# One core, two fused model blocks: how the tokens' quarters are laid over the partitions for the expert dots

## The chip, the cores and the metric

One core of a Trainium2 chip runs the whole program. The time is device microseconds of one execution, and a kernel's time is the median of its runs. The core has a tensor engine (PE: matrix products and turns, results in eight PSUM banks of 128 x 512 f32), a vector engine (VectorE, DVE), a scalar engine (ScalarE, ACT), GpSimd (POOL) and SyncE (SP), which work side by side and wait for each other by semaphores, and 16 DMA engines that move data between memory (HBM) and the on-chip SBUF.

## The reference, cut to what matters

256 tokens of width 1024 go through a first block of two layers and then a second block (latent attention and an mLSTM side by side, then a layer of experts). The change is in the experts:

```python
def one(xb):                                              # 128 tokens of h2, (128, 1024)
    q = (xb @ w_pq).reshape(128, 8, 2, 128)               # 8 heads, 2 halves
    s = einsum('thpd,hpkd->thpk', q, sub_keys)            # 128 scores per half
    sv, si = top_k(s, 16)                                 # then the best 16 of the 256 sums:
    best, pos = top_k(cand, 16); eidx = take(cidx, pos)   # 16 experts of 16384 per head and token
    g = softmax(best)
    act = gelu(einsum('thkd,td->thk', expert_u[eidx], xb))
    return einsum('thk,thkd->td', g * act, expert_v[eidx])
```

So each token meets 128 experts, and every expert row (u and v, 2 x 1024 f32, 8 KB) is fetched for one token. For 256 tokens that is 268 MB.

## The kernel before, in words

The tokens are two tiles of 128 (tt = 0 and 1). `first_*` and `mix_*` are the blocks up to the experts; `peer_*` is the expert part, one function per engine. Tile 0 enters the expert part while tile 1 is still in the mixers of the second block: `second_tile_at(g)` hands out tile 1's remaining steps, one or two with each batch g.

A turn k is one head of one tile (`TURNS`, 16 turns: heads 0 to 4 of tile 0, head 4 of tile 1, then both tiles by turns, at the end heads 0 to 3 of tile 1). For a turn PE makes the queries (`queries`, 16 products against `w_pq`) and the scores (`scores`, 2 products), each copied out of PSUM by ScalarE (`queries(k)` and `scores(k)` of `peer_scalar`), VectorE picks the best 16 (`halves`, `candidates`, `places`), PE spreads the list (`list_spread`) and VectorE copies it out (`listed`). GpSimd then gathers the expert rows with indirect DMAs (L3095). A turn has four batches of four gathers. One gather brings 128 rows of 8 KB, 1 MB, for 32 tokens: partition p of a gather belongs to token p % 32 of a quarter and to slot p // 32. Sixteen buffers `e_uv` are used in four places of four; places 2 and 3 come into use at batches 8 and 17 (`ROOM_AT`).

Each gather n of a batch is for quarter n of the tile's tokens. VectorE multiplies its u rows with the tokens and sums (`dots`, L2890), which needs the 32 tokens of a quarter repeated over the four groups of 32 partitions: these are the four tensors `m["h2q"][tt][q]`, each 128 x 1024. ScalarE makes gelu and a diagonal (`gelu`, `folded`, from the constant block `K["fold"]`), and PE adds the weighted v rows (`add`, `e_diag`).

The quarters come from `hT`, the normed tokens with the features on the partitions. `quarter_turned(tt, q)` (L2653) does for each half of the features 16 products of 128 x 32 by the identity, four for each of four feature tiles: each writes the same 32 tokens, turned, to one group of 32 partitions of a PSUM bank. `quarter_set` (L3004) copies the bank with ScalarE. For tile 0 three quarters stand in PE's order between the scores of turn 0 and the queries of turn 1, and the last one behind these (L2738 to L2742). For tile 1 they are the steps ("quarter", 0..3) of batches 15 to 18 (L2580); in a batch PE does them behind the batch's first add and ahead of the routing products that follow (L2758 to L2760). Tile 1's first turn is turn 5 (batches 20 to 23); its queries are in batch 14, its scores in batch 15, its list in batch 17. Turn 6's queries are in batch 17 behind the quarter, its scores in batch 18 behind the quarter, its list in batch 21 (`ROUTING_AT`). `dots` waits for the last copy of its quarter only in a tile's first turn (L2888).

The order of every engine's work is written out by hand in this way. Banks are taken in turn from a rotation (`c.banks.take`); PE waits until ScalarE or VectorE has emptied a bank. At the entry of the expert part the rotation is banks 2 and 3 (L1832), later 2, 3 and 7, from tile 1's output on again 2 and 3.

Of the kernel before, what the change touches and what calls it, by code (L numbers as in the profile page):

```python
# [57 lines left out]
def constants():  # L58

    p, f = np.arange(P)[:, None], np.arange(P)[None, :]  # L60
    t = np.arange(T).reshape(NT, P)
    n = np.arange(CMP_PAD)
    parts = {}
    parts["ident"] = np.eye(P)
    parts["zeros"] = np.zeros((P, P))
    parts["lower"] = np.where(f <= p, 0.0, NEG)
    parts["upper"] = np.where(f >= p, 0.0, NEG)
    ok = (n[None, None] < NCMP) & (n[None, None] * S_CMP + L_CMP - 1 <= t.T[:, :, None])
    parts["cmp_neg"] = np.where(ok, 0.0, NEG).reshape(P, -1)
    parts["cmp_one"] = ok.astype(float).reshape(P, -1)  # L70
    parts["blocks"] = (np.arange(P)[:, None] // CMP_PAD == np.arange(HEADS)[None]).astype(float)
    inv = (np.float32(10000.0) ** (-np.arange(0, HD, 2, dtype=np.float32) / np.float32(HD)))
    parts["inv_freq"] = np.broadcast_to(inv, (P, HD // 2))
    half = ROPE2 // 4
    inv2 = np.float32(10000.0) ** (-np.arange(half, dtype=np.float32) * np.float32(2.0 / (2 * half)))
    ang = np.stack([(t // 64).T, (t % 64).T], -1).astype(np.float32)[..., None] * inv2
    parts["cos2"] = np.cos(ang).reshape(P, -1)
    parts["sin2"] = np.sin(ang).reshape(P, -1)
    parts["fold"] = (np.arange(P)[:, None] % SIDE == np.arange(SIDE)[None]).astype(float)
    parts["iota"] = np.broadcast_to(np.arange(TOPK), (P, TOPK))  # L80
    parts["ones"] = np.ones((P, P))
    at, where = 0, {}
    for name, a in parts.items():
        where[name] = (at, at + a.shape[1])
        at += a.shape[1]
    return np.concatenate(list(parts.values()), 1).astype(np.float32), where
# [2486 lines left out]
def second_tile_at(g):  # L2573
    work = [("values", g - 1)] if 1 <= g <= MLA_H else []
    work += [("attention", g)] if g < MLA_H else []
    work += [("outputs", g - 4)] if 4 <= g < 4 + ML_H else []
    work += [("levels", g - 3)] if 3 <= g < 3 + ML_H else []
    return work + {5: [("att_out",)], 6: [("att_turn",)], 7: [("out0", 0)], 8: [("out0", 1), ("summed", 0)],
                   9: [("gated", 0), ("summed", 1)], 10: [("turn", 0), ("gated", 1)], 11: [("turn", 1), ("out1", 0)],
                   12: [("out1", 1), ("mixed",)], 13: [("normed",)], 14: [("filled",)], 15: [("quarter", 0)],  # L2580
                   16: [("quarter", 1)], 17: [("quarter", 2)], 18: [("quarter", 3)]}.get(g, [])


def peer_memory(nc, stack, second, cond):
# [14 lines left out]
def peer_tensor(c, m, mix, K):  # L2599
# [1 line left out]
    bank_k, bank_q = c.banks.tiles[0:2]  # L2601
    acc = [c.banks.tiles[4:6], c.banks.tiles[6:8]]
    hT, ident = m["hT"], K["ident"]


    in_keys = []

# [42 lines left out]
        spread(bank_k[:, 2 * P:2 * P + BUFS], m["best"][:, k % 2], ("weight_spread", k))  # L2650
        in_keys[:] = [("weight_set", k)]

    def quarter_turned(tt, q):  # L2653

        tokens = slice(tt * P + q * SIDE, tt * P + q * SIDE + SIDE)
        for half in range(2):
            bank = take("h2q", tt, q, half)
            for k in range(4):
                for s in range(QUARTERS):
                    pe.mm(bank[s * SIDE:s * SIDE + SIDE, k * P:k * P + P], hT[:, 4 * half + k, tokens], ident,  # L2660
                          skip_group_check=True, tile_position=(0, s * SIDE),
                          tell=filled("h2q", tt, q, half) if (k, s) == (3, QUARTERS - 1) else None)

    def add(g, c0, c1):

# [48 lines left out]
    def mixers_after(step, *a):  # L2714
# [3 lines left out]
        elif step == "attention":  # L2718
            later.att_turned(*a)
            if a[0] + 1 < MLA_H:  # L2720
                later.att_scores(a[0] + 1)
        elif step == "out0":
            if a[0] == 0:
                c.banks.rotate(2, 3)
            later.mix_out(0, range(2 * a[0], 2 * a[0] + 2))
        elif step == "out1":
            later.mix_out(1, range(2 * a[0], 2 * a[0] + 2))
        elif step == "quarter":
            quarter_turned(1, *a)

    c.banks.leave(0)
    c.banks.leave(1)
# [2 lines left out]
    kept_busy(c, K, bank_q, 512, 256)  # L2735
    queries(0)
    scores(0)
    for q in range(QUARTERS - 1):  # L2738
        quarter_turned(0, q)
    queries(1)  # L2740
    quarter_turned(0, QUARTERS - 1)
    scores(1)  # L2742
    list_spread(0)
    weights_spread(0)
# [215 lines left out]
def peer_scalar(c, m, mix, K, x):  # L2960
# [36 lines left out]
    def folded(g):  # L2997

        k, batch = divmod(g, PER_TURN)
        for n in range(BATCH):  # L3000
            slot = batch * BATCH + n
            act.f(m["fold_w"][:, g % 2, n, :], K["fold"], ACT.Copy, scale=m["weight"][:, k % 2, slot:slot + 1], settled=n == 0)

    def quarter_set(tt, q):  # L3004
        for half in range(2):
            act.wait_ge(*c.full("h2q", tt, q, half))
# [37 lines left out]
    def mixers_late(step, *a):  # L3044
# [2 lines left out]
            later.att_turned(*a)  # L3047
        elif step == "mixed":
            later.squares()
        elif step == "quarter":  # L3050
            quarter_set(1, *a)

    first.filled(m["hT"], 0)
    queries(0)
    scores(0)
    for q in range(QUARTERS - 1):
        quarter_set(0, q)
    soft(0)
    queries(1)
    quarter_set(0, QUARTERS - 1)  # L3060
    scores(1)
    weighted(0)
    folded(0)
# [66 lines left out]
def parts_of(nc, keep, A, out, counted):  # L3130
# [3 lines left out]
    table = nc.alloc_sbuf_tensor("constants", [P, max(b for _, b in where.values())], F32)[:]  # L3134
    K = {name: table[:, a:b] for name, (a, b) in where.items()}
    zeros = where["zeros"][0]
    K["masks"] = table[:, zeros + P:zeros + 3 * P].rearrange("p (d t) -> p d t", d=2)
    K["wide"] = table[:, 0:4 * P]
    K["mask2"] = table[:, zeros:zeros + 2 * P]
# [106 lines left out]
```

## Time and profile before

| | us |
|---|---|
| median of 3 runs | 1372.97 (1371.43 to 1375.32) |
| profiled execution | 1378.54 |
| its span | 1377.1 |
| PE busy (share of the span) | 1031.6 (75%) |
| VectorE busy | 885.6 (64%) |
| ScalarE busy | 475.3 (35%) |
| GpSimd busy | 307.3 (22%) |
| gathers' queue, share of 16 DMA engines | 46.5%, 268.45 MB |

The profile is of one execution. Its times count from the span's start; the expert part begins at some 672 us. A busy share is an average over stages with different limits. In a row of a timeline the first number is the start, the second the time until the last of the merged instructions ended, then the engine, the line (often that of a helper, L169 for all products), the operation, what it writes and reads, the sizes, and in brackets how long the engine had been idle and what ended that. One f32 product leaves two MATMUL records, one turn leaves one. "issue" is idle time in which the engine waited for nothing that the profile shows; "remote" is a wait whose releaser the profile doesn't name.

### The profile page before, as it was taken

To read this page: it belongs to the slowest core of one execution; us is meant where nothing else is said; L and a number is where in the kernel's file an instruction comes from. 1 tells how busy PE (TensorE), PEld (TensorE's weight loads), DVE (VectorE), ACT (ScalarE), POOL (GpSimd) and SP (SyncE) were. 2 spreads that over 40 slices of the span, in tenths; PEclk is the share of its full clock that TensorE was granted. 3 is DMA by queue.
4 is the path that set the end of the run, shared out by engine and by line. 5 is a ranking of instruction groups with operands and counts; after the bars stand their busy time and mean duration, and the time that the engine had idled before them with its cause. 6 is when DMAs were issued, how large, how long until landed. Compare 5 with 4: busy or idle time off the path is not lost.

```text
span 1377.1 us, 17655 instructions
## 1 busy us (share of the span) xinstructions
PE 1031.6 (75%) x6291; PEld 590.1 (43%) x6291; DVE 885.6 (64%) x2281; ACT 475.3 (35%) x1312; POOL 307.3 (22%) x265
## 2 busy tenths in 40 slices
PE   7998999999899999999968787665434455443535
PEld 4776756577675647445534431332212222211201
DVE  5488643429864445845476798458866777777755
ACT  2013623101352521465347654333332233233321
POOL 0000000000000000000044444344435555443451
PEclk9999999999999999999989898876666666666667
DMA  8362453436237332145189999999999999999997
GB/s 305 132 223 92 160 214 130 183 105 249 93 131 281 117 104 93 62 183 203 55 358 426 409 426 427 425 412 368 426 426 426 426 426 426 427 426 426 427 426 306
DMA packets 56107, 391.14 MB, mean 284 GB/s; under 512 B 9931, under 2 KB 13055, under 8 KB 15955
## 3 DMA queue, kind: packets, MB, share of 16 engines
q0 software_dynamic: 37440, 268.45, 46.5%
q1 hardware_dynamic: 18578, 121.56, 23.9%
q8 instruction: 50, 0.82, 0.2%
q14 instruction: 39, 0.31, 0.1%
HBM read 387.89 MB, written 1.05 MB: 282 GB/s over the span
## 4 chain that ended last, share of the span: by engine, by line
DVE 21%; PE 16%; DMA 12%; ACT 5%; another core or an unknown queue 4%; issue 4%; POOL 1%; ACTq 0%; DVEq 0%
PE bank L169 16%; DMA e_uv<-in_experts_dram,e_listed 9%; DVE e_uv L2890 8%; DMA e_uv<-in_experts_dram,e_listed_uv 2%; DVE e_hot L185 1%; POOL e_uv L3095 1%; ACT e_diag L230 1%; DVE e_rest L2821 1%; ACT L230 1%; DVE e_e L210 1%; ACT m_W L230 1%; PE bank L174 1%; DMA m_w<-in_ada_dram 1%; DVE e_si L2825 1%
## 5 line engine op out<-in xcount | busy, mean ns | idle before, releaser
L3095 POOL DMA_INDIRECT e_uv<-in_experts_dram,e_listed x252 | 296.8, 1178 | 1035.3 <-DVE e_listed L202 806.9
L169 PE MATMUL bank<-e_uv,e_diag 128*32 128x512 f32 x1024 | 231.1, 879 | 285.0 <-ACT e_diag L230 254.5
L2890 DVE CUSTOM_DVE_ANT_0 e_uv<-e_uv,e_h2q 128x1024 f32<-128x1024 f32 x192 | 228.4, 1224 | 63.8 <-DMA e_uv<-in_experts_dram,e_listed 59.5
L169 PEld LDWEIGHTS bank<-e_uv,e_diag 128*32 128x32 f32 x1024 | 41.4, 140 | 409.7 <-ACT e_diag L230 283.5
L169 PE MATMUL bank<-hT,weights 128*128 128x256 f32 x640 | 141.0, 380 | 2.8 <-DVE hT L191 1.4
L169 PEld LDWEIGHTS bank<-hT,weights 128*128 128x128 f32 x640 | 120.8, 190 | 21.0 <-DVE hT L191 1.6
L230 ACT ACT_TABLE_LOAD x79 | 101.4, 1283 | 7.8 <-PE bank L169 1.7
L169 PE MATMUL bank<-weights,hT 128*128 128x512 f32 (+1 forms) x256 | 102.5, 557 | 1.7 <-DMA weights<-in_layer_q_dram 1.7
L197 DVE SCALAR_TENSOR_TENSOR conv<-ubuf,vec,conv 128x256 f32<-128x256 f32 x240 | 96.8, 480 | 0.6
L230 ACT ACTIVATE e_act<-e_dot 128x4 f32<-128x4 f32 (+1 forms) x81 | 16.6, 205 | 210.0 <-DVE e_dot L2890 200.7
L169 PE MATMUL bank<-weights,mixT 128*128 128x512 f32 x192 | 85.5, 598 | 2.4 <-DVE mixT L202 1.6
L2890 DVE CUSTOM_DVE_ANT_0 e_uv<-e_uv,e_hT 128x1024 f32<-128x1024 f32 x64 | 76.3, 1222 | 13.1 <-DMA e_uv<-in_experts_dram,e_listed 13.1
L169 PEld LDWEIGHTS bank<-e_hT,e_w_pq 128*128 128x128 f32 x512 | 62.0, 201 | 18.7 <-issue 18.2
L169 PEld LDWEIGHTS bank<-weights,hT 128*128 128x128 f32 x256 | 48.8, 194 | 49.4 <-issue 44.1
L230 ACT ACTIVATE e_diag<-cond_mod_rows,e_act 128x32 f32<-128x32 f32 x256 | 63.1, 311 | 8.1
L169 PE MATMUL bank<-e_hT,e_w_pq 128*128 128x128 f32 x512 | 65.2, 288 | 0.6 <-ACT e_hT L230 0.6
L2817 DVE MAX8 e_sv<-cond_mod_rows 128x8 f32<-128x128 f32 x32 | 9.4, 295 | 86.8 <-ACT cond_mod_rows L234 69.5
L230 ACT ACTIVATE cond_mod_rows<-constants,e_weight 128x32 f32<-128x32 f32 x256 | 61.3, 310 | 2.1
L169 PEld LDWEIGHTS bank<-weights,mixT 128*128 128x128 f32 x192 | 35.5, 190 | 45.4 <-issue 42.5
L185 DVE TENSOR_TENSOR x_sb<-bank,x_sb 128x512 f32<-128x512 f32 x16 | 11.1, 692 | 63.4 <-PE bank L169 63.4
L230 ACT ACTIVATE S<-S,mx 128x128 f32<-128x128 f32 (+1 forms) x64 | 29.1, 455 | 61.5 <-DVE mx L222 59.3
L169 PE MATMUL bank<-m_w,e_hT 128*128 128x464 f32 (+1 forms) x96 | 40.0, 569 | 1.2 <-PEq L3169 1.1
(385 smaller groups left out, 1429.5 us busy)
## 6 DMA issues: line engine op xcount, KB each, us to landing
weights<-in_ada_dram SPq DMA_DIRECT2D x8, 2048.0 KB, 8.7
weights<-in_layer_out_dram SPq DMA_DIRECT2D x6, 2048.0 KB, 8.1
e_w_pq<-in_w_pq_dram SPq DMA_DIRECT2D x12, 1024.0 KB
weights<-in_layer_cmp_dram SPq DMA_DIRECT2D x4, 2048.0 KB, 8.3
weights<-in_layer_q_dram SPq DMA_DIRECT2D x2, 2048.0 KB, 8.8
weights<-in_layer_kvc_dram SPq DMA_DIRECT2D x2, 2048.0 KB, 12.7
weights<-in_layer_gb_dram SPq DMA_DIRECT2D x2, 2048.0 KB, 15.1
weights<-in_layer_ga_dram SPq DMA_DIRECT2D x2, 2048.0 KB, 15.2
```

The source lines that it names most:

```text
L169: ins = self.engine.matmul(out, lhsT, rhs, start=start, stop=stop, **kw)
L174: ins = self.engine.transpose(out, a, ident)
L185: return self.mark(self.engine.tensor_tensor(out, a, b, op), tell)
L197: return self.mark(self.engine.scalar_tensor_tensor(out, a, s, b, op0, op1), tell)
L210: return self.mark(self.engine.tensor_reduce(out, a, AX.X, op), tell)
L230: return self.mark(self.engine.activation(out, a, func, **kw), tell)
L2817: dve.mark(c.nc.vector.max(out_v[:, 0:8], values))
L2821: dve.mark(c.nc.vector.match_replace(scratch, out_v[:, 0:8], values, -3e38))
L2825: return dve.mark(c.nc.vector.max_index(out_i[:, 8:16], out_v[:, 8:16], scratch))
L2890: dve.mark(c.nc.vector.tensor_tensor_reduce(u, u, h2q[tt][n], 1.0, 0.0, MUL, ADD, m["dot"][:, j:j + 1]), ("dots_set", g, c0) if n == c1 - ...
L3095: ins = c.nc.gpsimd.indirect_dma_start(out=to, out_offset=None, in_=rows, in_offset=bass.IndirectOffsetOnAxis(ap=of, axis=0))
```

## The change

The tile is turned back whole, once: `tokens_turned(tt)` makes eight 128 x 128 turns from `hT` into two banks, and ScalarE (`tokens_set`) copies them to `h2q[tt][3]`, the place of the last quarter. Then `quarter_spread(tt, q)` makes each half of each quarter with one product: the 32 token rows of the quarter (32 partitions, 512 columns) by 32 rows of a constant block that has a one wherever column and row agree modulo 32. The products of quarter 0 wait for ScalarE's copies. The constant block grows from 32 to 128 columns; `K["fold"]` is its first 32. In tile 1's steps batch 15 now has ("rows",) and the four quarters follow in batches 16 to 19. For tile 0 the rotation is set to banks 2, 3 and 7 ahead of the turns, two quarters stand ahead of the queries of turn 1 and two behind them, on PE and ScalarE alike.

```diff
--- before.py
+++ after.py
@@ -76,7 +76,7 @@
     ang = np.stack([(t // 64).T, (t % 64).T], -1).astype(np.float32)[..., None] * inv2
     parts["cos2"] = np.cos(ang).reshape(P, -1)
     parts["sin2"] = np.sin(ang).reshape(P, -1)
-    parts["fold"] = (np.arange(P)[:, None] % SIDE == np.arange(SIDE)[None]).astype(float)
+    parts["fold"] = (np.arange(P)[:, None] % SIDE == np.arange(P)[None] % SIDE).astype(float)
     parts["iota"] = np.broadcast_to(np.arange(TOPK), (P, TOPK))
     parts["ones"] = np.ones((P, P))
     at, where = 0, {}
@@ -2577,8 +2577,8 @@
     work += [("levels", g - 3)] if 3 <= g < 3 + ML_H else []
     return work + {5: [("att_out",)], 6: [("att_turn",)], 7: [("out0", 0)], 8: [("out0", 1), ("summed", 0)],
                    9: [("gated", 0), ("summed", 1)], 10: [("turn", 0), ("gated", 1)], 11: [("turn", 1), ("out1", 0)],
-                   12: [("out1", 1), ("mixed",)], 13: [("normed",)], 14: [("filled",)], 15: [("quarter", 0)],
-                   16: [("quarter", 1)], 17: [("quarter", 2)], 18: [("quarter", 3)]}.get(g, [])
+                   12: [("out1", 1), ("mixed",)], 13: [("normed",)], 14: [("filled",)], 15: [("rows",)],
+                   16: [("quarter", 0)], 17: [("quarter", 1)], 18: [("quarter", 2)], 19: [("quarter", 3)]}.get(g, [])
 
 
 def peer_memory(nc, stack, second, cond):
@@ -2601,7 +2601,7 @@
     bank_k, bank_q = c.banks.tiles[0:2]
     acc = [c.banks.tiles[4:6], c.banks.tiles[6:8]]
     hT, ident = m["hT"], K["ident"]
-
+    h2_rows = [m["h2q"][tt][QUARTERS - 1] for tt in range(NT)]
 
     in_keys = []
 
@@ -2650,16 +2650,23 @@
         spread(bank_k[:, 2 * P:2 * P + BUFS], m["best"][:, k % 2], ("weight_spread", k))
         in_keys[:] = [("weight_set", k)]
 
-    def quarter_turned(tt, q):
-
-        tokens = slice(tt * P + q * SIDE, tt * P + q * SIDE + SIDE)
+    def tokens_turned(tt):
+
+        for half in range(2):
+            bank = take("h2_rows", tt, half)
+            for k in range(4):
+                pe.turn(bank[:, k * P:k * P + P], hT[:, 4 * half + k, tt * P:tt * P + P], ident,
+                        tell=filled("h2_rows", tt, half) if k == 3 else None)
+
+    def quarter_spread(tt, q):
+
+        tokens = slice(q * SIDE, q * SIDE + SIDE)
         for half in range(2):
             bank = take("h2q", tt, q, half)
-            for k in range(4):
-                for s in range(QUARTERS):
-                    pe.mm(bank[s * SIDE:s * SIDE + SIDE, k * P:k * P + P], hT[:, 4 * half + k, tokens], ident,
-                          skip_group_check=True, tile_position=(0, s * SIDE),
-                          tell=filled("h2q", tt, q, half) if (k, s) == (3, QUARTERS - 1) else None)
+            if q == 0:
+                pe.wait_ge(*c.taken("h2_rows", tt, half))
+            pe.mm(bank[:, :], K["spread"][tokens, :], h2_rows[tt][tokens, half * 512:half * 512 + 512],
+                  tell=filled("h2q", tt, q, half))
 
     def add(g, c0, c1):
 
@@ -2725,8 +2732,10 @@
             later.mix_out(0, range(2 * a[0], 2 * a[0] + 2))
         elif step == "out1":
             later.mix_out(1, range(2 * a[0], 2 * a[0] + 2))
+        elif step == "rows":
+            tokens_turned(1)
         elif step == "quarter":
-            quarter_turned(1, *a)
+            quarter_spread(1, *a)
 
     c.banks.leave(0)
     c.banks.leave(1)
@@ -2735,10 +2744,13 @@
     kept_busy(c, K, bank_q, 512, 256)
     queries(0)
     scores(0)
-    for q in range(QUARTERS - 1):
-        quarter_turned(0, q)
+    c.banks.rotate(2, 3, 7)
+    tokens_turned(0)
+    quarter_spread(0, 0)
+    quarter_spread(0, 1)
     queries(1)
-    quarter_turned(0, QUARTERS - 1)
+    quarter_spread(0, 2)
+    quarter_spread(0, 3)
     scores(1)
     list_spread(0)
     weights_spread(0)
@@ -3001,6 +3013,12 @@
             slot = batch * BATCH + n
             act.f(m["fold_w"][:, g % 2, n, :], K["fold"], ACT.Copy, scale=m["weight"][:, k % 2, slot:slot + 1], settled=n == 0)
 
+    def tokens_set(tt):
+        for half in range(2):
+            act.wait_ge(*c.full("h2_rows", tt, half))
+            act.copy(m["h2q"][tt][QUARTERS - 1][:, half * 512:half * 512 + 512], c.banks.tile("h2_rows", tt, half),
+                     tell=c.banks.emptied("h2_rows", tt, half))
+
     def quarter_set(tt, q):
         for half in range(2):
             act.wait_ge(*c.full("h2q", tt, q, half))
@@ -3047,17 +3065,21 @@
             later.att_turned(*a)
         elif step == "mixed":
             later.squares()
+        elif step == "rows":
+            tokens_set(1)
         elif step == "quarter":
             quarter_set(1, *a)
 
     first.filled(m["hT"], 0)
     queries(0)
     scores(0)
-    for q in range(QUARTERS - 1):
-        quarter_set(0, q)
+    tokens_set(0)
+    quarter_set(0, 0)
+    quarter_set(0, 1)
     soft(0)
     queries(1)
-    quarter_set(0, QUARTERS - 1)
+    quarter_set(0, 2)
+    quarter_set(0, 3)
     scores(1)
     weighted(0)
     folded(0)
@@ -3134,6 +3156,7 @@
     table = nc.alloc_sbuf_tensor("constants", [P, max(b for _, b in where.values())], F32)[:]
     K = {name: table[:, a:b] for name, (a, b) in where.items()}
     zeros = where["zeros"][0]
+    K["spread"], K["fold"] = K["fold"], K["fold"][:, 0:SIDE]
     K["masks"] = table[:, zeros + P:zeros + 3 * P].rearrange("p (d t) -> p d t", d=2)
     K["wide"] = table[:, 0:4 * P]
     K["mask2"] = table[:, zeros:zeros + 2 * P]
```

## Rows read from the trace of the kernel before

**Rows 1.** the page: GB/s moved in each of 40 slices of 34.4 us
```profile
GB/s 305 132 223 92 160 214 130 183 105 249 93 131 281 117 104 93 62 183 203 55 358 426 409 426 427 425 412 368 426 426 426 426 426 426 427 426 426 427 426 306
```

**Rows 2.** busy time by window: engines (x instructions), PE clock, DMA share, GB/s
```profile
906.00:912.00 6.00, 4.89 (x62) 2.08 (x64) 6.00 (x12) 1.23 (x6) 4.71 (x4) 0.62 0.93 367
948.00:954.00 6.00, 2.85 (x16) 0.59 (x16) 5.90 (x12) 2.12 (x9) 3.37 (x2) 0.50 0.45 150
```

**Rows 3.** timeline of PE at the entry: start us, length us, instruction, [idle before]
```profile
671.47 1.09 PE L174 MATMUL bank<-constants,m_W 128*128 128x128 f32 x8 [0.23 <-DVE m_W L191]
679.22 4.21 PE L169 MATMUL bank<-constants,e_hT 128*32 128x128 f32 x143
684.76 1.58 PE L169 MATMUL bank<-constants,e_hT 128*32 128x128 f32 x49 [1.33 <-issue]
686.26 3.84 PE L169 MATMUL bank<-e_hT,e_w_pq 128*128 128x128 f32 x32
690.03 1.96 PE L169 MATMUL bank<-constants,e_hT 128*32 128x128 f32 x64
692.56 0.43 PE L169 MATMUL bank<-e_e,constants 128*32 128x4 f32 x32
694.81 1.12 PE L169 MATMUL bank<-m_krT,m_qrT 64*128 64x512 f32 x2
695.87 3.70 PE L169 MATMUL bank<-m_w,e_hT 128*128 128x512 f32 x8
```

**Rows 4.** timeline of ScalarE and VectorE in the same stretch
```profile
680.37 0.58 ACT L234 COPY e_hT<-bank 128x512 f32<-128x512 f32 x1 [0.67 <-PE bank L169]
688.33 0.21 ACT L230 ACTIVATE e_best<-e_gap 128x16 f32<-128x16 f32 x1
...
690.39 0.17 DVE L197 SCALAR_TENSOR_TENSOR e_e<-e_e 128x16 f32<-128x16 f32 x1
```

**Rows 5.** timeline of ScalarE and VectorE, batches 15 to 19
```profile
884.87 0.37 ACT L234 COPY cond_mod_rows<-bank 128x256 f32<-128x256 f32 x1
...
917.19 0.37 ACT L234 COPY e_qT<-bank 128x256 f32<-128x256 f32 x1 [0.73 <-PE bank L169]
928.72 0.37 ACT L234 COPY cond_mod_rows<-bank 128x256 f32<-128x256 f32 x1 [0.67 <-PE bank L169]
...
929.12 0.29 DVE L2817 MAX8 e_sv<-cond_mod_rows 128x8 f32<-128x128 f32 x1 [13.72 <-ACT cond_mod_rows L234]
```

**Rows 6.** timeline of PE, batches 14 to 19
```profile
860.95 1.97 PE L174 MATMUL bank<-constants,m_W 128*128 128x128 f32 x8
...
880.22 2.22 PE L169 MATMUL bank<-constants,e_hT 128*32 128x128 f32 x52
...
910.52 1.87 PE L169 MATMUL bank<-constants,e_hT 128*32 128x128 f32 x48
913.31 3.84 PE L169 MATMUL bank<-e_hT,e_w_pq 128*128 128x128 f32 x32
918.82 1.59 PE L169 MATMUL bank<-constants,e_hT 128*32 128x128 f32 x40
931.50 3.37 PE L169 MATMUL bank<-e_uv,e_diag 128*32 128x512 f32 x16 [2.82 <-ACT e_diag L230]
```

**Rows 7.** timeline of VectorE and GpSimd, batch 20 and turn 6's first gather
```profile
939.66 1.21 DVE L2890 CUSTOM_DVE_ANT_0 e_uv<-e_uv,e_h2q 128x1024 f32<-128x1024 f32 x1
...
950.33 1.74 POOL L3095 DMA_INDIRECT e_uv<-in_experts_dram,e_listed  x1 [8.64 <-DVE e_listed L202]
```

**Rows 8.** timeline of ScalarE in two later turns, query copy and score copy
```profile
1039.84 0.37 ACT L234 COPY e_qT<-bank 128x256 f32<-128x256 f32 x1 [3.38 <-PE bank L169]
...
1051.34 0.37 ACT L234 COPY cond_mod_rows<-bank 128x256 f32<-128x256 f32 x1
...
1157.94 0.37 ACT L234 COPY e_qT<-bank 128x256 f32<-128x256 f32 x1 [2.73 <-PE bank L169]
...
1164.99 0.37 ACT L234 COPY cond_mod_rows<-bank 128x256 f32<-128x256 f32 x1
```

## The prediction, made before the changed kernel was run

> **What bounds the kernel now.** I read the slices of the page first. From the 21st slice on (688 us) the DMA engines move 409 to 427 GB/s with one break, the 28th slice with 368 [rows 1]: the second half is the stream of expert rows that GpSimd gathers. It can end earlier in two ways only: it starts earlier, or it stands still for less time. So I asked windows where it stands still. There are two pockets: 906 to 912 at 367 GB/s and 948 to 954 at 150 GB/s [rows 2]. Against 426 they lose 6 x 59/426 = 0.8 us and 6 x 276/426 = 3.9 us, 4.7 us together. From the 29th slice to the 39th the rate is flat at 426 or 427.
>
> Then the timelines, to see what ends each wait of the gathers. The start: the first list of experts is spread by PE at 692.56 [rows 3], but VectorE had chosen the experts at 690.39 + 0.17 = 690.56 [rows 4]. PE was late by 2.0 us, since it ran tile 0's quarters, the queries and the scores of turn 1 first. The large pocket: GpSimd's first gather of turn 6 starts at 950.33 after 8.64 us of waiting for the list [rows 7]. Behind that list is one unbroken VectorE chain that began at 929.12 after 13.72 us of idling for the scores of turn 6 [rows 5], and those come from PE behind quarter 3. That quarter, 64 PE records, 1.96 us when undisturbed [rows 3], starts at 918.82 with 40 records [rows 6] and its scores are copied only at 928.72. The small pocket has the same form a turn earlier: quarter 0 starts at 880.22 in earnest [rows 6], the scores of turn 5 are copied at 884.87 [rows 5].
>
> **The entry, tile 0.** Before: 679.22 to 692.56 is 13.34 us [rows 3]. Quarters 0 to 2 with the gap of 1.33 us take 7.04, the queries 3.77 start to start, the last quarter and the scores 2.53. After: eight turns of 128x128 cost 1.09 us [rows 3]. The first spread waits for ScalarE to copy the first turned half, 0.58 us [rows 4]; half the turns are done after 0.55, so the copy ends 1.13 + about 0.25 of handing over after 679.22, some 0.3 us behind the turns. Then eight products, 32 rows deep, 128 columns out and 512 long. No row shows this shape. From below: four products of 512 columns in 3.70 us, less the tail of the last of some 0.26, is 0.86 each; from above: the product with 64 rows starts at 694.81 and the next one at 695.87, 1.06 each [rows 3]. A short depth earns nothing in these rows. I take 0.90, nearer to the run of like products, since both halves of a quarter are alike: 7.2 us. Note that this is about what a half cost before (1.96/2 = 0.98): the change removes PE records, 512 to 32 for the quarters of both tiles with 16 turns beside them, but hardly any PE time. Sum: 1.09 + 0.3 + 7.2 + 3.77 + 0.64 for the scores = 13.0, a gain of 0.3 us. At 0.86 it is a gain of 0.7, at 1.06 a loss of 0.9. The gap of 1.33 us, in which PE waited for nothing that the trace names, is left out of the new sum because the record-dense stretch in which it fell is gone; if it comes back, the entry loses 1.0 instead. The gain cannot pass 1.8 us, where VectorE's choice at 690.56 becomes the last one.
>
> ScalarE makes two more copies of 0.58 per tile. In the entry it idles before each copy [rows 4], so they are hidden, but its order now decides something: quarters 2 and 3 are copied behind the exponential of turn 0 (done at 688.6 [rows 4]) and behind the query copy. There are three banks for four spreads, so the fourth spread cannot start before about 689.8. By the sum PE reaches it at about 690.5: hidden, with 0.7 us of cover, and late next if PE got much faster.
>
> The Trainium skill, page "TensorE: Matmul & The Clock Gate", section "Part 3: Packing small matmuls — row/col tiling", says that products at different row groups run side by side in the array. Here the second half of a quarter and the first of the next would pair; no row of this trace has two neighbouring products at different row groups, so it neither agrees nor disagrees.
>
> **Tile 1, turn 5.** Batch 15 had quarter 0 in front of the scores: 880.22 to 883.83, 3.6 us [rows 6]. Now eight turns stand there, 1.09 us [rows 3] or 1.97 us when the granted clock is low [rows 6]; two ScalarE copies follow as before. That is 1.6 to 2.5 us on PE. ScalarE's two copies of the turned halves and the score copy follow within a microsecond of it. I take 1.5 us, since the few records after 882.4 came slowly for a reason that may stay (below: 0). From that copy on VectorE's chain to this list is unbroken, so list 5 moves by 1.5 and the small pocket of 0.8 us closes.
>
> **Tile 1, turn 6.** Three parts. First the 1.5 us are inherited, as the dots, the diagonals and the adds that precede the queries hang on the same chain. Second, batch 17 had quarter 2 in front of the queries, 910.52 to 913.31 or 2.8 us [rows 6]; quarter 1 now stands there as two spreads, 1.8 us at the high clock, twice that at half clock: a gain of 1.0 (bounds -0.8 and +1.1). Third, from the query copy to the score copy 917.19 to 928.72 is 11.5 us [rows 5]. The seven later turns to 1207 us have no quarter in this place, and still show 7.05 us in the shortest (1157.94 to 1164.99) and 11.50 in the longest (1039.84 to 1051.34) [rows 8]: the slow piece belongs mostly to the turn, not to the quarter. The middle of the two is 9.3; a quarter's two spreads remain in front of the scores, so I take 10.0, a gain of 1.5 (bounds: 0, and 4.5 at 7.05). Together the list of turn 6 comes 1.5 + 1.0 + 1.5 = 4.0 us earlier. The stream itself ran 0.8 us ahead, so 3.2 us of the second pocket's 3.9 close.
>
> **Moved and added.** Quarter 3 goes from batch 18 to 19 and the first dots of tile 1, in batch 20, need it. The fourth dot started at 939.66 [rows 7]. The new place is behind batch 19's add, 931.50 + 3.37 = 934.9 [rows 6]; two spreads at half clock, 1.8 each, end at 938.5 and ScalarE's last copy at 939.1. So it is just in time with nothing else moved; all of it moves together. Cover: 0.5 us. Queued behind on PE is only batch 20's add; on ScalarE it is the next exponential, which VectorE needs 4 us later. The wait of quarter 0 for the whole tile's copy is met a batch earlier, at nothing. The constants grow by 96 columns, 48 KB, 0.1 us at 426 GB/s at the kernel's start: counted as lost. ScalarE's weight fold reads the first 32 columns as before: nothing.
>
> **Sum.** 0.3 + 0.8 + 3.2 - 0.1 = 4.2 us. The profiled execution took 1378.54 us (span 1377.1), so it becomes 1374.3. It lies 5.6 us above the median of 1372.97; the pockets may be a little smaller in an execution without the profiler, but I have no row for that. Forecast: 1372.97 - 4.2 = 1368.8 us.
>
> **Rivals.**
> *Nothing is given back.* The slow piece is the turn's own and ScalarE and PE come out of it at the same instants. For it: 11.50 us in a turn without a quarter. Against it: the shortest of 7.05, and 3.6 us for quarter 0 where eight turns need 2. Only 0.3 at the entry and little elsewhere: 1372.4.
> *Everything is given back.* The spreads pair up in the array, which takes some 1.7 us (two of 0.86) off the eight and brings the entry to the bound of 1.8, and both pockets close: 1372.97 - 1.8 - 4.7 = 1366.5. That is what the page's rule of the row groups would make of the entry (by it the trace is silent).
> *Slower: the last quarter becomes the wait.* Spreads at 1.06 lose 0.9 at the entry, and the slow piece of a turn falls on batch 19's spreads, which have 0.5 us of cover. From there each microsecond holds the fourth dot of batch 20, list 6 behind it and the stream. Such a piece lasts up to 6 us; at 3 us the time is 1372.97 + 0.9 + 3 + 0.1 = 1377.0. It decides as soon as PE reaches quarter 3 later than about 935.5 on the old clock of events while the scores came no earlier.
>
> **Chances.** Forecast 0.45, nothing 0.25, everything 0.14, slower 0.16. About 0.3%, 4.1 us, is what a measurement of this kernel can tell from no change. Over half of the forecast's own spread (1366.5 to 1371.5) lies beyond it. Faster: 0.26 + 0.14 = 0.40; slower: 0.14 of the last case; the rest, 0.46, is the same within 0.3%. The range that leaves out 2 in 10 goes from 1365.0 to 1376.0.
>
> **What would show it.** Right: eight PE turns of some 1.1 us at 679 and no gap behind them; spreads 0.86 to 0.95 us apart; first list spread near 692.2; scores of turn 5 copied near 883.4 and of turn 6 near 924.5 on the same scale; 948 to 954 at over 400 GB/s. Wrong: spreads over 1.0 us apart; VectorE waiting for a copy of quarter 3 in batch 20; the score copy of turn 6 still 11 us behind its query copy; or the pocket closed and the end not earlier, which would say that the stream isn't what sets the end.

## The result: 1.006 times the time before, and the profile after

| | before | after |
|---|---|---|
| median, us | 1372.88 (1371.43 to 1375.32, 6 runs) | 1381.64 (1381.01 to 1382.56, 6 runs) |
| ratio after to before, 95% interval | | 1.006 (1.0049 to 1.007) |
| profiled execution, its span | 1378.54, 1377.1 | 1381.07, 1379.7 |
| mean granted clock of PE | 0.866 | 0.860 |

The forecast was 1368.8 us with a range of 1365 to 1376. The kernel is slower by 8.8 us, outside of the range and on the other side of no change.

From the page of the changed kernel: the GB/s in 40 slices, and the gathers' queue with its packets, MB and share of 16 DMA engines:

```profile
GB/s 306 138 216 92 167 211 126 183 114 240 93 142 270 116 122 75 62 183 220 58 376 420 405 421 422 420 421 420 421 421 421 421 420 420 421 419 422 421 421 275
...
q0 software_dynamic: 37440, 268.45, 47.0%
```

From the 24th slice to the 39th the rate is 419 to 422 GB/s, where [rows 1] had 425 to 427 outside of the pockets. The queue moves the same packets and bytes and holds the engines for 47.0% of a longer span (46.5% before). The 28th slice, with 368 in [rows 1] the visible pocket, now shows 420, like its neighbours. The windows of the changed kernel, with the columns of [rows 2]:

```profile
906.00:912.00 6.00, 3.54 (x48) 1.53 (x40) 3.39 (x5) 2.68 (x8) 4.06 (x4) 0.81 1.02 419
948.00:954.00 6.00, 0.00 (x0) 0.00 (x0) 1.31 (x4) 0.73 (x4) 2.76 (x3) 0.72 1.02 417
1000.00:1300.00 300.00, 133.31 (x1152) 57.67 (x1148) 211.35 (x521) 85.92 (x301) 123.43 (x113) 0.66 1.01 421
```

and of the kernel before, two windows that were not shown ahead of the prediction:

```profile
930.00:964.00 34.00, 17.69 (x164) 7.70 (x164) 28.15 (x69) 10.85 (x38) 17.06 (x12) 0.68 0.91 368
...
1000.00:1300.00 300.00, 133.82 (x1208) 58.45 (x1197) 214.31 (x543) 90.19 (x316) 140.32 (x120) 0.66 1.01 426
```

So both pockets of [rows 2] are closed (367 to 419 and 150 to 417 GB/s), as forecast, and the end is not earlier. (Whether it was the new order of work that closed them is a question of its own: see b_pad384 below.) The last window says why: over 300 us in which only the expert part is left, the DMA engines are as full (share 1.01 in both), and move 421 GB/s where they moved 426. The stream is 268.45 MB: at 426 GB/s 630 us, at 421 GB/s 638 us. These 7.5 us are most of the 8.8.

The entry of tile 0, PE of the changed kernel:

```profile
678.60 1.04 PE L174 MATMUL bank<-constants,e_hT 128*128 128x128 f32 x8
679.90 2.92 PE L169 MATMUL bank<-e_h2q,constants 32*128 32x512 f32 x8 [0.26 <-ACT e_h2q L234]
682.74 3.84 PE L169 MATMUL bank<-e_hT,e_w_pq 128*128 128x128 f32 x32
686.51 2.92 PE L169 MATMUL bank<-e_h2q,constants 32*128 32x512 f32 x8
689.36 0.71 PE L169 MATMUL bank<-e_keysT,e_qT 128*128 128x128 f32 x4
690.10 0.43 PE L169 MATMUL bank<-e_e,constants 128*32 128x4 f32 x32
...
695.45 4.98 PE L169 MATMUL bank<-m_w,e_hT 128*128 128x512 f32 x8
```

The sum of the prediction, term by term: turns and copy 679.90 - 678.60 = 1.30 us (1.39 forecast); four spreads 682.74 - 679.90 = 2.84 us (3.6 forecast), four more 2.85; the queries 3.77 (3.77); the scores 0.74 (0.64). From the turns to the list spread 11.50 us, where [rows 3] have 13.34: a gain of 1.8 us, the bound that the prediction gave, and not 0.3. There is no gap. The spreads take 0.71 us each on average, below the lower bound of 0.86: two products that lie on different groups of 32 rows overlap. The single records behind the merged row 686.51 show it: two products begin at 686.51 and 686.52, only 0.01 us apart, while the records of the gate's 128-row products in [rows 3] never start less than 0.43 us apart. By the Trainium skill, page "TensorE: Matmul & The Clock Gate", section "Part 3: Packing small matmuls — row/col tiling", small products in distinct row groups run at the same time. The trace agrees as far as four products in 2.84 us against four in 3.70 [rows 3] go.

GpSimd of the changed kernel at the entry; the value in brackets is the idle time before the gather and who ended it:

```profile
691.15 1.09 POOL L3117 DMA_INDIRECT e_uv<-in_experts_dram,e_listed  x1 [690.70 <-DVE e_listed L202]
...
700.70 1.31 POOL L3117 DMA_INDIRECT e_uv<-in_experts_dram,e_listed  x1 [4.72 <-PE bank L169]
```

The first gather starts at 691.15, 2.4 us earlier than the 693.53 of the profile before. The fifth starts at 700.70, later than the 699.84 of before. It needs a buffer whose memory the output gate's product still reads (the PE row 695.45 above, 4.98 us; 3.70 in [rows 3]). PE's clock in 3 us windows of the changed kernel (columns: PE busy and instructions, granted clock, DMA share, GB/s):

```profile
688.00:691.00 3.00, 2.50 (x40) 1.00 0.72 303
691.00:694.00 3.00, 2.99 (x35) 0.54 0.55 126
694.00:697.00 3.00, 3.00 (x4) 0.50 0.95 380
697.00:700.00 3.00, 3.00 (x7) 0.83 0.99 421
```

After 12 us of nearly unbroken work the granted clock goes from its upper level (1.00, 2.4 GHz) to its lower one (0.50, 1.2 GHz) between 691.0 and 691.5, stays there until 698, and the products behind the entry pay: what the spreads gained is given back before the fifth gather.

Tile 1, ScalarE of the changed kernel (query copy and score copy of turn 5, the same of turn 6, last copy of quarter 3), then the first gathers of both lists on GpSimd:

```profile
868.92 0.37 ACT L234 COPY e_qT<-bank 128x256 f32<-128x256 f32 x1
...
872.83 0.37 ACT L234 COPY cond_mod_rows<-bank 128x256 f32<-128x256 f32 x1
...
904.81 0.37 ACT L234 COPY e_qT<-bank 128x256 f32<-128x256 f32 x1 [0.82 <-PE bank L169]
...
909.58 0.37 ACT L234 COPY cond_mod_rows<-bank 128x256 f32<-128x256 f32 x1 [0.16 <-PE bank L169]
...
918.92 0.59 ACT L234 COPY e_h2q<-bank 128x512 f32<-128x512 f32 x1 [0.27 <-PE bank L169]
```

```profile
894.35 1.74 POOL L3117 DMA_INDIRECT e_uv<-in_experts_dram,e_listed  x1 [15.24 <-DVE e_listed L202]
...
933.54 0.94 POOL L3117 DMA_INDIRECT e_uv<-in_experts_dram,e_listed  x1 [9.79 <-DVE e_listed L202]
```

The scores of turn 5 are copied 3.9 us behind their queries' copy, those of turn 6 4.8 us (11.5 in [rows 5]). The first gather of turn 6 is issued at 933.54, not 950.33 as in [rows 7]. Quarter 3 is there at 919.5. The first four dots of tile 1 start at 919.43 to 922.87, and only the fourth needs it: no wait. After them the dots wait for landings, not for lists:

```profile
951.82 1.23 DVE L2902 CUSTOM_DVE_ANT_0 e_uv<-e_uv,e_h2q 128x1024 f32<-128x1024 f32 x1 [3.74 <-DMA e_uv<-in_experts_dram,e_listed]
```

### The profile page after: what moved, and what is told of

Read it like the earlier page. It is cut to its first block, busy times and chain, and to the rows that moved or that the text cites. A ratio compares the mean times of both kernels' runs of the same rounds, so it can differ in the third digit from the quotient of the medians.

```text
span 1379.7 us, 16736 instructions
## 1 busy us (share of the span) xinstructions
PE 1034.6 (75%) x5827; PEld 583.3 (42%) x5827; DVE 890.5 (65%) x2281; ACT 478.2 (35%) x1317; POOL 289.6 (21%) x265
## 3 DMA queue, kind: packets, MB, share of 16 engines
q0 software_dynamic: 37440, 268.45, 47.0%
## 4 chain that ended last, share of the span: by engine, by line
DMA 30%; PE 14%; DVE 8%; ACT 5%; POOL 4%; issue 2%; ACTq 0%; DVEq 0%
DMA e_uv<-in_experts_dram,e_listed 28%; PE bank L169 13%; POOL e_uv L3117 4%; DVE e_uv L2902 3%; DMA e_uv<-in_experts_dram,e_listed_uv 2%; ACT e_diag L230 1%; ACT m_W L230 1%; ACT L230 1%; DMA m_w<-in_ada_dram 1%; PE bank L174 0%; ACT e_h2q L230 0%; DVE m_ctx L185 0%; ACT e_hT L230 0%; DVE m_W L185 0%; DVE e_rest L2833 0%
## 5 line engine op out<-in xcount | busy, mean ns | idle before, releaser
L3117 POOL DMA_INDIRECT e_uv<-in_experts_dram,e_listed x252 | 278.9, 1107 | 1055.3 <-DVE e_listed L202 809.9
L169 PE MATMUL bank<-e_uv,e_diag 128*32 128x512 f32 x1024 | 234.0, 895 | 301.5 <-ACT e_diag L230 301.4
L234 ACT COPY PT<-bank 128x256 f32<-128x256 f32 (+2 forms) x36 | 16.4, 456 | 49.8 <-PE bank L174 47.1
```

Of the source, the lines that this page charges most:

```text
L169: ins = self.engine.matmul(out, lhsT, rhs, start=start, stop=stop, **kw)
L234: return self.mark(self.engine.copy(out, a), tell)
L3117: ins = c.nc.gpsimd.indirect_dma_start(out=to, out_offset=None, in_=rows, in_offset=bass.IndirectOffsetOnAxis(ap=of, axis=0))
```

## The experiments

Theory P (place): the 8 KB rows of the gathers land more slowly because the buffers moved. The constants grew by 96 columns, 384 bytes per partition, so everything allocated behind them moved by 384 bytes. The gather buffers (8192 bytes each, one behind the other) started at byte 79360 of each partition, 310 x 256, and start at 79744 now, 128 past a multiple of 256. Rival M (mechanism): the new order of work itself slows the stream or lengthens the chain. Rival C: the longer constant array as it lies in the chip's memory and its load. The recorded expectations call what is not P theory Q.

Every experiment was timed beside the kernel before on its chip: 1375.32 us median for the first four, 1376.55 for a_tile0, a_tile1, a_best and b_pad32 (29 runs each). The ratios and their intervals are as recorded; they need not be the quotient of the two medians. A ratio below 1 is faster than the kernel before.

**a_place: the changed kernel, its gather buffers back at 79360.** Three small tensors are laid over constants that nobody needs any more:

```diff
-            ..., ("weight", [P, 2, BUFS], F32), ("sv", [P, 2, TOPK], F32), ("si", [P, 2, TOPK], U32),
-            ("sif", [P, 2, TOPK], F32), ("best", [P, 2, TOPK], F32), ...
+            ..., ("si", [P, 2, TOPK], U32),
+            ("best", [P, 2, TOPK], F32), ...
...
+        for name, kept in (("weight", "cmp_neg"), ("sv", "cmp_one"), ("sif", "inv_freq")):
+            second[name] = K[kept].rearrange("p (a s) -> p a s", a=2)
```

> The changed kernel, with three small tensors of the expert part (weight, sv, sif, 384 bytes per partition) laid over three parts of the constants that are no longer read, so that the gather buffers start at byte 79360 of each partition as in the kernel before, and not at 79744. Theory P (place of the gather buffers: the stream fell from 426 to 421 GB/s because their start moved by 384 bytes): the stream is back at 426 GB/s, the first gather still starts near 691.2, the time is 1370 to 1373. Theory Q (the new products themselves, or the larger constant array in memory, slow the stream): 421 GB/s stays and the time is 1380 to 1382.

Measured: 1373.41 us (12 runs), ratio 0.9989 (0.9977 to 1.0000). Windows of this kernel:

```profile
930.00:964.00 34.00, 19.41 (x164) 8.18 (x154) 25.69 (x60) 12.08 (x40) 19.45 (x15) 0.65 0.99 402
...
1000.00:1300.00 300.00, 134.18 (x1164) 56.97 (x1164) 219.86 (x549) 92.47 (x320) 139.92 (x118) 0.65 1.01 426
```

426 GB/s again, and the loss is gone: 1.006 / 0.9989 is 1.007, some 10 us (between two comparisons, each against its own runs of the kernel before). M falls, since all of the change's work is still in this kernel. So does the load of the longer constant array, the second half of C, for it is still in here too. The profile also shows the lower clock and a late fifth gather behind an early first one:

```profile
691.57 1.09 POOL L3117 DMA_INDIRECT e_uv<-in_experts_dram,e_listed  x1 [691.12 <-DVE e_listed L202]
...
702.68 0.94 POOL L3117 DMA_INDIRECT e_uv<-in_experts_dram,e_listed  x1 [6.29 <-PE bank L169]
```

**b_pad384: the kernel before, its gather buffers moved by 384 bytes.** Nothing else changes:

```diff
-            ..., ("norm", [P, 2], F32)):
+            ..., ("norm", [P, 2], F32), ("pad", [P, 96], F32)):
```

> The kernel before, with 384 unused bytes per partition ahead of the gather buffers (start 79744), nothing else. Theory P: 421 GB/s in the gather stage and 1380 to 1383 us, slower than before by 8 to 9. Theory Q: 1372 to 1374, no change.

Measured: 1383.01 us (4 runs), ratio 1.0052 (1.0035 to 1.0069).

```profile
930.00:964.00 34.00, 17.99 (x164) 7.88 (x156) 26.40 (x61) 9.29 (x32) 18.24 (x14) 0.75 1.01 418
948.00:954.00 6.00, 4.77 (x21) 1.80 (x22) 6.00 (x12) 3.09 (x14) 4.98 (x3) 0.50 1.02 422
...
1000.00:1300.00 300.00, 135.81 (x1162) 59.29 (x1165) 211.29 (x526) 89.75 (x313) 132.39 (x118) 0.67 1.01 421
```

An unused tensor of 96 columns costs 7 us and takes the rate to the 421 GB/s of the changed kernel. With a_place this shows P from both sides. The pad also moves the mixers' tensors, which lie over the same memory, but in this window those are done, and the buffer of `w_pq`, the other load of the stage, lies ahead of the pad. Tile 1's quarters lie behind the gather buffers and move along; only VectorE reads them, which is busy for 211 of the 300 us, while the DMA engines are full (1.01) in both kernels.

The first two windows tell a reader to be careful with the result above. This kernel has the old quarters in the old order, and yet its profile has no pocket either: 418 GB/s where the kernel before had 368, and 422 where it had 150. So the closed pockets of the changed kernel's profile can't be put down to the change alone. The times say the same: with the buffers at 79744 the old quarters take 1.0052 of the kernel before and the new ones 1.006, so no gain of the change is to be seen there.

**b_pad256: the same pad with 64 columns**, `("pad", [P, 64], F32)`: the buffers start at 79616, again a multiple of 256.

> The kernel before, with 256 unused bytes per partition ahead of the gather buffers (start 79616, which 256 divides and 512 does not). Theory P in the form that a multiple of 256 bytes is what counts: 426 GB/s, 1372 to 1374. In the form that it is 512: 421 GB/s, 1380 to 1383. Theory Q: 1372 to 1374.

Measured: 1374.96 us (10 runs), ratio 0.9996 (0.9983 to 1.0009).

```profile
948.00:954.00 6.00, 3.90 (x17) 0.93 (x18) 5.90 (x12) 2.33 (x10) 4.11 (x3) 0.55 0.55 197
1000.00:1300.00 300.00, 135.22 (x1208) 58.26 (x1200) 215.23 (x545) 91.05 (x319) 146.59 (x122) 0.69 1.01 424
```

A shift by itself is harmless: the place within 256 bytes counts. The 384 bytes of the changed kernel shift it by half of that. (The 424 holds one dip at 1032 to 1041 us; the slices around it are at 426.)

**b_hbm: the kernel before, its constant array 96 columns longer in the chip's memory only.**

```diff
-    c.sp.load(table[:, P:], A["constants"][:, P:], "constants_in", 0)
+    c.sp.load(table[:, P:], A["constants"][:, P:920], "constants_in", 0)
...
-    laid = [("constants", constants()[0]), ...
+    laid = [("constants", np.concatenate([constants()[0], np.zeros((P, 96), np.float32)], 1)), ...
```

> The kernel before, with 96 unused columns more in the constant array in memory (48 KB, as in the changed kernel); SBUF is laid out as before and the extra columns are not loaded. If the place of the expert rows in memory is what slows the stream: 421 GB/s and 1380 to 1383 us. Theory P: 1372 to 1374.

Measured: 1375.44 us (10 runs), ratio 1.0002 (0.999 to 1.0013).

```profile
948.00:954.00 6.00, 6.00 (x44) 3.81 (x36) 6.00 (x13) 1.16 (x5) 5.31 (x3) 0.81 0.95 366
1000.00:1300.00 300.00, 136.16 (x1164) 59.95 (x1164) 219.43 (x546) 91.10 (x316) 137.01 (x118) 0.68 1.01 426
```

The first half of C falls, the place of the arrays in memory. The first window tells something else: the same order of work as before shows 366 GB/s here, 197 in b_pad256 and 150 in [rows 2]. The depth of the large pocket varies from one execution to the next, and of these three the profile that the prediction used had the deepest.

**b_pad32: a pad of 8 columns**, `("pad", [P, 8], F32)`: the buffers start at 79392, 32 bytes past a multiple of 256. It tells whether the cost grows with the distance.

> The kernel before with 32 unused bytes per partition ahead of the gather buffers (start 79392, 32 past a multiple of 256). If any start off a multiple of 256 bytes costs the stream the same: 421 GB/s between 1000 and 1300 us and 7 to 8 us slower. If the cost grows with the distance past the multiple (32 of 256 against the 128 of the changed kernel): 425 GB/s and about 2 us.

Measured: 1386.39 us (4 runs), ratio 1.0068 (1.005 to 1.0087).

```profile
1000.00:1300.00 300.00, 134.66 (x1156) 59.73 (x1160) 211.40 (x528) 89.84 (x313) 134.70 (x118) 0.65 1.01 419
```

Neither expectation was met, it costs more than both: at least as much as 128 bytes off, so the cost does not grow with the distance (268.45 MB at 419 GB/s is 641 us, 10.5 more than at 426; the ratio gives 9.4). Both starts off the multiple cost, both starts on one do not.

**a_tile0: only tile 0's part of the change, buffers at 79360.** a_place with tile 1's quarters as before, `quarter_turned` put back for them:

```diff
-                   12: [("out1", 1), ("mixed",)], 13: [("normed",)], 14: [("filled",)], 15: [("rows",)],
-                   16: [("quarter", 0)], 17: [("quarter", 1)], 18: [("quarter", 2)], 19: [("quarter", 3)]}.get(g, [])
+                   12: [("out1", 1), ("mixed",)], 13: [("normed",)], 14: [("filled",)], 15: [("quarter", 0)],
+                   16: [("quarter", 1)], 17: [("quarter", 2)], 18: [("quarter", 3)]}.get(g, [])
...
-            quarter_spread(1, *a)
+            quarter_turned(1, *a)
```

> The changed kernel with the gather buffers back at byte 79360, and of the change only tile 0's part: tile 1's quarters are made by the old 32-column products in batches 15 to 18. Theory E (what is left of a gain comes from the entry, where the first gather started 2 us earlier): first gather near 691.5 us, time 1.5 to 2 us under the kernel before. Theory L (it comes from the lists of turns 5 and 6 in tile 1's batches): no gain, within 0.5 us of the kernel before, though the first gather is early.

Measured: 1375.54 us (12 runs, 1371.31 to 1380.63), ratio 0.9995 (0.998 to 1.0009).

```profile
690.60 1.08 POOL L3128 DMA_INDIRECT e_uv<-in_experts_dram,e_listed  x1 [690.16 <-DVE e_listed L202]
...
696.91 1.63 POOL L3128 DMA_INDIRECT e_uv<-in_experts_dram,e_listed  x1 [1.50 <-PE bank L169]
```

In the profile the clock stays up (1.00 in each 3 us window from 691 to 700) and the fifth gather is 2.9 us earlier than before, yet over twelve runs no gain can be told from nothing. Nor is one refuted: the interval reaches from 2.8 us faster to 1.2 us slower, and the 1.5 to 2 us of theory E lie in it. The profiled execution was the fastest of the twelve, so it may be one in which the clock did not fall.

**a_tile1: only tile 1's part, buffers at 79360.** a_place with tile 0's quarters as before, ScalarE's copies likewise:

```diff
-    tokens_turned(0)
-    quarter_spread(0, 0)
-    quarter_spread(0, 1)
+    for q in range(QUARTERS - 1):
+        quarter_turned(0, q)
     queries(1)
-    quarter_spread(0, 2)
-    quarter_spread(0, 3)
+    quarter_turned(0, QUARTERS - 1)
```

> The changed kernel with the gather buffers back at byte 79360, and of the change only tile 1's part: tile 0's quarters are made by the old products between scores and list. Theory E: first gather near 693.5, time within 0.5 us of the kernel before. Theory L: 1.5 to 4 us faster, with no window under 400 GB/s between 930 and 964 us.

Measured: 1375.19 us (12 runs), ratio 0.9981 (0.9971 to 0.9991), some 2.6 us; the two medians alone are only 1.4 us apart. Query copy and score copy of turns 5 and 6 on ScalarE, and the window of the pocket:

```profile
873.32 0.37 ACT L234 COPY e_qT<-bank 128x256 f32<-128x256 f32 x1
...
879.42 0.37 ACT L234 COPY cond_mod_rows<-bank 128x256 f32<-128x256 f32 x1
...
911.24 0.37 ACT L234 COPY e_qT<-bank 128x256 f32<-128x256 f32 x1 [0.82 <-PE bank L169]
...
921.14 0.37 ACT L234 COPY cond_mod_rows<-bank 128x256 f32<-128x256 f32 x1
```

```profile
930.00:964.00 34.00, 16.29 (x158) 7.32 (x160) 24.10 (x59) 14.01 (x46) 18.75 (x15) 0.65 1.01 417
```

Of the two parts this is the one whose gain is clear of nothing, though the intervals of both overlap. In the profile it pays where the prediction said: 930 to 964 at 417 GB/s instead of 368. The expectation that no window there would be under 400 GB/s was missed: 948 to 954 has 393.

**a_best: the whole change, with the gather buffers and also the weight buffers at multiples of 256.** a_place with `("pad0", [P, 8])` ahead of `w_pq`, `("pad1", [P, 8])` at the end, and 48 columns ahead of the first block's tensors:

```diff
+    nc.alloc_sbuf_tensor("pad", [P, 48], F32)
     cond = c.cond = condition_memory(nc, keep)
```

> The changed kernel with three small tensors laid over dead constants, and three paddings that start the four weight buffers of the layers, the query weights of the experts and the gather buffers at multiples of 256 bytes. The gather stream at 426 GB/s as with the buffers at 79360. If the start matters for every load that runs while the DMA engines are full, the 12 MB of query weights save another 0.4 us; the layers' weights load at 90 to 200 GB/s beside a busy PE and should save nothing. 1.5 to 2.5 us under the kernel before.

Measured: 1373.7 us (12 runs), ratio 0.9981 (0.9969 to 0.9993).

```profile
930.00:964.00 34.00, 14.85 (x148) 7.64 (x148) 22.16 (x51) 11.51 (x41) 18.56 (x15) 0.67 1.00 410
...
1000.00:1300.00 300.00, 132.87 (x1164) 58.57 (x1164) 214.71 (x547) 92.34 (x320) 148.48 (x117) 0.69 1.01 424
```

```profile
691.00:694.00 3.00, 2.79 (x37) 1.00 0.43 104
694.00:697.00 3.00, 3.00 (x8) 1.00 0.93 371
```

Its gather buffers start at 79616, as in b_pad256. It is 0.19% faster than the kernel before, and cannot be told from a_place (0.9989) or a_tile1; so nothing is shown for the weight buffers. In this profile the clock does not fall behind the same spreads that were followed by the lower level in the changed kernel's and a_place's.

## Why the prediction was wrong, step by step

**The step that failed** is the one that stood in half a sentence: "The constants grow by 96 columns, 48 KB, 0.1 us at 426 GB/s at the kernel's start: counted as lost." It counted the bytes that are loaded and not the place of what is allocated behind them. b_pad384 gives the term: 0.0052 x 1375 = 7.2 us (4.8 to 9.5), not 0.1; within the changed kernel a_place puts it at about 10. No rival contained it, so the range did not either. The rate that every term was reckoned against, 426 GB/s, was taken as given by the chip. It was a property of where the buffers lay. (Its reading of [rows 1] was too smooth besides: the 21st slice has 358 GB/s, not 409 or more, and the 23rd, with 409, was priced nowhere.) The last thing that the prediction said would prove it wrong happened: "the pocket closed and the end not earlier". The reading attached to it, that the stream isn't what sets the end, was wrong too: the stream sets it and had become slower.

**The entry: right in sign, 0.3 us forecast, 1.8 measured** (11.50 against 13.34 us). The term that was mis-sized is the spread, 0.90 taken, 0.71 measured. The rival "everything is given back" had this right in kind: it took 1.7 us off the eight for products that pair up, and eight took 5.69 us where eight of 0.86 are 6.88, 1.2 us less. The gap of 1.33 us did not come back. But in two of the four profiles with these spreads the lower clock behind them gave the gain back by the fifth gather (in the six with tile 0's old quarters the clock stayed up until 700), and a_tile0's ratio of 0.9995 (0.998 to 1.0009) neither shows a gain in the time nor rules one out. The prediction followed the chain up to the first gather. The stream does not start in earnest before the fifth, which waits for PE again.

**Turn 5: right.** Forecast 1.5 us earlier, from a shorter piece ahead of the scores. From query copy to score copy the profiles with tile 1's old quarters have 7.6 to 8.1 us (kernel before, a_tile0, b_hbm, b_pad256, b_pad384, b_pad32), those with the new ones and the buffers in place 6.0 to 6.3 (a_tile1 6.10): 1.8 us.

**Turn 6: right where the stream runs at its old rate.** Forecast from query to score copy: 11.5 before, 10.0 after. With the old quarters five profiles have 11.3 to 12.6 (b_pad384 7.7, with a wait of 4.3 us ahead of the query copy instead), with the new ones a_tile1 has 9.9, a_place 10.2, a_best 11.3. The changed kernel's own 4.8 is the exception, and since a_place and a_best do the same work in the same order, it is not the change alone that gives it. What the spreads cut on PE shows in a_place as a new wait of ScalarE. PE, then ScalarE:

```profile
918.77 0.43 PE L169 MATMUL bank<-e_best,constants 128*32 128x4 f32 x32
919.14 0.71 PE L169 MATMUL bank<-e_keysT,e_qT 128*128 128x128 f32 x4
```

```profile
915.12 0.37 ACT L234 COPY e_qT<-bank 128x256 f32<-128x256 f32 x1 [0.81 <-PE bank L169]
...
918.88 0.59 ACT L234 COPY e_h2q<-bank 128x512 f32<-128x512 f32 x1 [0.27 <-issue]
925.06 0.17 ACT L234 COPY constants<-bank 128x16 f32<-128x16 f32 x1 [5.60 <-remote]
925.32 0.37 ACT L234 COPY cond_mod_rows<-bank 128x256 f32<-128x256 f32 x1
```

PE ends the scores at 919.85, in good time beside the 928.72 at which the kernel before copied them [rows 5]. But ScalarE stands still from 919.47 to 925.06 for something that the profile calls "remote", 5.6 us of it, and copies the scores only then. a_best has 6.7 us and a_tile1 5.3 us of this wait at the same place. So the rival's claim that "the slow piece is the turn's own" was half right: a piece of 5 to 7 us fell on PE before and falls on ScalarE after. In each of these profiles the queue named "instruction" moves one packet in this stretch: in the microsecond from 920 in the kernel before, from 914 in a_best, from 918 in a_tile1, and in a_place (queue: packets, MB, share of 16 engines, 920 to 921 us):

```profile
q8 instruction: 1, 0.02, 5.8%
```

In the changed kernel's own profile the packet passes at 910, when the scores were copied already. That the engine waits for its instructions behind the gathers' packets fits this; no run tested it. The Trainium skill, page "Runtime: NRT & Kernel Launch", section "Instruction fetch mechanics", has each engine fetch its program in blocks of 16 KiB by a DMA queue of its own, hidden by the pace at which instructions are issued. The size agrees with the row; that it is hidden is in doubt here, where the engines are full of gathers.

**The pockets: right in kind, too large in size.** Forecast: 4.0 us of 4.7 given back. In the window 930 to 964 the loss against 426 GB/s was 34 x 58/426 = 4.6 us in the profile before, 3.7 in a_tile0, 3.4 in b_pad256 and 2.2 in b_hbm; with tile 1's new part 0.7 in a_tile1, 1.9 in a_place, 1.3 in a_best. On average 3.5 against 1.3: 2.2 us, which fits a_tile1's ratio (2.6 us, between 1.2 and 4.0). These are the kernels with the buffers at a multiple of 256. Off it the old quarters lose 0.2 us in b_pad384 (418 against 421) and 2.2 in b_pad32 (392 against 419). The prediction noted that it had one profiled execution, 5.6 us above the median, and still charged its pocket in full.

**The slower rival**, that the last quarter becomes the wait, did not happen: its copy ends at 919.51 and the fourth dot starts at 922.87.

**All together:** without the shift the change gains 1.5 to 2.6 us (0.9989 and 0.9981) where 4.2 were forecast; a_place's interval reaches to no gain at all. The shift by itself costs 7.2 us (4.8 to 9.5) in the kernel before. That makes some 5 us slower, with ends at 2 and 8, and 6.7 to 9.6 were measured (the interval of the ratio). The ranges meet, but the shift seems to cost the changed kernel some 2 us more than the kernel before. One reading fits: in b_pad384's profile the slower stream has no pocket left that the change could close, so the change's gain is gone as well. It rests on one profile, and b_pad32's still has a pocket (309 GB/s from 948 to 954), so it is not shown.

**Open:** why the clock fell behind the spreads in two profiles and not in two others; whether a_tile0's early start is lost in most executions by it (the two profiled executions that kept the clock were the fastest of their twelve, a_place's lay 2.2 us above its median, but the changed kernel's own was the second fastest of six); what "remote" stands for; why turns 5 and 6 went so fast in the changed kernel's own profile.

## What to carry to other kernels

When a diff makes a tensor larger, list what is allocated behind it and where it starts now; here 384 bytes in a block of constants cost 7 to 10 us, several times what the change gained. In a stage that is bound by transfers, compare its GB/s over a long undisturbed window before any wait: 426 to 421 pointed at the stream at once, while the waits for both of tile 1's lists had become shorter. And a pocket that one profiled execution shows is worth its average over several, not its depth in that one.

## What the runs showed of the hardware

- **The start of the buffers in a partition sets the rate of the gathers.** Rows of 8 KB, DMA engines full: 426 GB/s with a start at 79360, 424 to 426 at 79616 (both multiples of 256), 421 at 79744 (128 past one), 419 at 79392 (32 past one). All buffers are 8192 bytes apart, so all share the place. 32 bytes past is no cheaper than 128 past. The Trainium skill, page "DMA: Bandwidth & Descriptors", section "How a descriptor splits into AXI transactions", says that what starts off a 256-byte boundary needs one more transaction, since its first one begins at the boundary below; it speaks of reads. An estimate from that page: 33 transactions instead of 32 for a row, up to 3%. The runs agree in kind and show 1.2 to 1.6%. In b_pad384, b_pad256 and b_pad32 nothing lies elsewhere in memory than in the kernel before, so the side that moved is the one that is written; that the extra transaction arises there is argued, not shown.
- **Products of 32 rows on different row groups overlap:** with 512 columns four take 2.84 us, 0.71 each, against 0.86 for like products with 128 rows, and two of them start 0.01 us apart.
- **A stretch of PE can be followed by the lower clock in one execution and not in another:** 0.50 from about 691.2 us in the changed kernel and in a_place, 1.00 in a_best and a_tile0 after the same work, and 1.00 up to 700 us in all six profiles with tile 0's old quarters, in which PE had stood idle for 1.3 to 1.5 us between 682 and 687.
